# A two-layer hybrid backbone on one core: in the first layer's experts the down product also keeps its weights stationary, its result is turned back, and the expert loop is rotated by a third of gate and up

## The reference, cut to what matters

```python
def ec_moe(h, w_router, w_e_gate, w_e_up, w_e_down):
    cap = EC_CAPACITY * t // N_EXPERTS
    aff = jax.nn.softmax((h @ w_router).astype(jnp.float32), axis=-1)
    vals, idx = lax.top_k(jnp.swapaxes(aff, 1, 2), cap)
    xs = jax.vmap(lambda hb, ib: hb[ib])(h, idx)
    hid = jax.nn.silu(jnp.einsum('becd,edf->becf', xs, w_e_gate)) * jnp.einsum('becd,edf->becf', xs, w_e_up)
    ys = jnp.einsum('becf,efd->becd', hid, w_e_down) * vals[..., None].astype(h.dtype)
    return jax.vmap(lambda yb, ib: jnp.zeros((t, d), yb.dtype).at[ib.reshape(-1)].add(yb.reshape(-1, d)))(ys, idx)
```

## Time and profile before

| | us |
|---|---|
| median of 3 runs (4555.68 to 4568.88) | 4561.98 |
| the profiled execution, its own time | 4566.59 |
| its span in the trace | 4564.6 |
| first expert product of the first layer, start | 1644.95 |
| last expert product of the first layer ends | 2486.25 |

### The profile page before, as it was taken

The page is one execution under the profiler, slowest core; times in us unless marked ns, Lnnn a source line. Parts: engine busy times, 40 slices in busy tenths (PEclk is TensorE's granted clock), DMA queues, the critical chain, the costliest instruction groups (busy, mean ns, idle before and its releaser), DMA issues.

```text
span 4564.6 us, 62566 instructions
## 1 busy us (share of the span) xinstructions
PE 3719.1 (81%) x25844; PEld 2530.3 (55%) x25844; DVE 1174.9 (26%) x2798; ACT 730.7 (16%) x1485; POOL 111.0 (2%) x166
## 2 busy tenths in 40 slices
PE   6699888888989569999997568898878947877785
PEld 3355674656776347776775345655556634444442
DVE  0332321425640231111110243323246131110111
ACT  2221222002211200000000221312022120010101
POOL 0000000000000000000000000000000000000000
PEclk9799898898999679999999678898878969999997
DMA  4172101001011159999997200110100219999996
GB/s 175 64 272 80 39 33 51 10 24 41 24 51 56 46 206 341 345 347 345 339 348 268 81 23 24 58 46 28 42 24 24 79 74 332 378 383 381 380 374 255
DMA packets 326203, 740.21 MB, mean 162 GB/s; under 512 B 7456, under 2 KB 79136, under 8 KB 325936
## 3 DMA queue, kind: packets, MB, share of 16 engines
q1 hardware_dynamic: 314704, 695.29, 41.8%
q0 software_dynamic: 11360, 43.05, 3.3%
HBM read 713.09 MB, written 25.21 MB: 162 GB/s over the span
## 4 chain that ended last, share of the span: by engine, by line
PE 64%; DMA 16%; DVE 11%; ACT 5%; issue 3%; DVEq 0%; ACTq 0%; SPq 0%; POOL 0%; POOLq 0%
PE bank L526 11%; PE bank L910 8%; PE bank L464 7%; PE bank L883 7%; PE bank L457 5%; DMA ring<-in_w_e_up 4%; PE bank L874 4%; DMA ring<-in_w_e_gate 4%; PE bank L800 3%; ACT work L986 3%; DMA ring<-in_w_e_down 3%; DVE work L1401 3%; PE bank L616 3%; DMA f_rows<-work,idx 3%; PE bank L528 2%
## 5 line engine op out<-in xcount | busy, mean ns | idle before, releaser
L526 PE MATMUL bank<-HT,ring 128*128 128x256 f32 x2560 | 636.7, 405 | 16.8 <-DVEq L1442 12.6
L526 PEld LDWEIGHTS bank<-HT,ring 128*128 128x128 f32 x2560 | 516.5, 205 | 133.5 <-issue 39.5
L874 PE MATMUL bank<-ring,work 128*64 128x256 f32 x1536 | 391.3, 414 | 129.7 <-DMA ring<-in_w_e_up 67.6
L910 PE MATMUL bank<-ring,work 128*96 128x512 f32 (+1 forms) x1408 | 468.0, 598 | 25.8 <-DMA ring<-in_w_e_down 24.3
L883 PE MATMUL bank<-work,ring 128*64 128x96 f32 x11264 | 483.7, 249 | 3.7 <-DVEq L1921 3.0
L883 PEld LDWEIGHTS bank<-work,ring 128*64 128x64 f32 x11264 | 477.3, 139 | 16.6 <-issue 16.0
L875 PE MATMUL bank<-ring,work 128*64 128x256 f32 (+1 forms) x1536 | 375.7, 385 | 0.0
L874 PEld LDWEIGHTS bank<-ring,work 128*64 128x64 f32 x1536 | 221.5, 149 | 270.9 <-DMA ring<-in_w_e_up 85.9
L471 PE MATMUL bank<-const,work 128*128 128x128 f32 (+1 forms) x828 | 155.9, 338 | 233.9 <-DVEq L1429 52.8
L910 PEld LDWEIGHTS bank<-ring,work 128*96 128x96 f32 (+1 forms) x1408 | 166.0, 150 | 291.5 <-issue 255.4
L464 PE MATMUL bank<-ring,HT 128*128 128x512 f32 (+2 forms) x960 | 309.1, 486 | 0.0
(11 more groups left out here) (165 smaller groups left out, 3331.8 us busy)
## 6 DMA issues: line engine op xcount, KB each, us to landing
ring<-in_w_e_gate SPq DMA_DIRECT2D x64, 2048.0 KB, 10.5
ring<-in_w_e_up SPq DMA_DIRECT2D x64, 2048.0 KB, 10.1
ring<-in_w_e_down SPq DMA_DIRECT2D x64, 2048.0 KB, 9.7
ring<-in_w_ada SPq DMA_DIRECT2D x24, 2048.0 KB, 8.1
ring<-in_w_e_gate SPq DMA_DIRECT2D x32, 1536.0 KB, 10.1
ring<-in_w_e_up SPq DMA_DIRECT2D x32, 1536.0 KB, 8.2
ring<-in_w_e_down SPq DMA_DIRECT2D x32, 1536.0 KB, 10.0
ring<-in_w_gate SPq DMA_DIRECT2D x16, 2048.0 KB, 8.5
```

The lines of the kernel that those rows point to most:

```text
L526: pe.matmul(b[:, 0:256], w[:, k, d4 * P:(d4 + 1) * P], HT[:, k, off:off + 256], start=(k == 0), stop=(k == KD - 1))
L874: pe.matmul(b[0:64, 0:256], e_xs[:, k, 0:64], w[:, k, 0:256], start=(k == 0), stop=(k == KD - 1))
L910: ins = pe.matmul(banks[6 + half][lo:lo + cap, :], e_hidT[:, at, 0:cap], w[:, k, half * 512:half * 512 + 512], start=(f == 0), stop=(f == ...
```

## The change

Only the first layer's expert stage changes; the second layer's code is taken apart from it and issues what it issued.

- **Down.** `wide_down` keeps the weights stationary, like gate and up: for 8 output blocks `m` and 11 hidden blocks `f`, two halves of 64 columns, with the 96 tokens moving. The result comes out turned: output feature on the partitions, 4 x 96 columns in each of banks 6 and 7. It is 352 matmul records where there were 44.
- **Turning back.** ScalarE and VectorE copy the two banks (128x384 each) to `e_yT`, which lies over the unused `e_hid`. `turn_y` makes 8 transposes (stationary 128x96, moving 128x128) into banks 4 and 5, and from there the scaled copies to `e_ys` are as before.
- **Rotation.** Gate and up of group 0 of expert 0 stand ahead of the loop. A pass is: gate and up 1, `choose`, gate and up 2, `turn_rows`, down 0 to 2, gate and up 0 of the *next* expert, `turn_y`. VectorE and ScalarE are rotated alike.

```diff
+                def pairs(b, c0, w, k, c, x, start, stop):
+                    for half in range(2):
+                        ins = pe.matmul(b[64 * half:64 * half + 64, c0:c0 + cap], w[:, k, c + 64 * half:c + 64 * half + 64], x,
+                                        start=start, stop=stop, skip_group_check=True)
+                    return ins
...
+                def wide_down(e, i):
+                    wpiece(e, 6 + i)
+                    kk = EXP_DOWN[i]
+                    w = slot(n0 + 6 + i, 1024, kk)
+                    for m in range(KD):
+                        for k in range(kk):
+                            f = 4 * i + k
+                            ins = pairs(banks[6 + m // 4], (m % 4) * cap, w, k, m * P, e_hidT[:, f, 0:cap],
+                                        f == 0 and m % 4 == 0, f == NF - 1)
+                    ins.then_inc(sems["ys"], 1)
+                def turn_y():
+                    pe.wait_ge(sems["yt_a"], c.nth("yt_a"))
+                    pe.wait_ge(sems["yt_d"], c.nth("yt_d"))
+                    pe.wait_ge(sems["ys_a"], c.nth("ys_a"))
+                    pe.wait_ge(sems["ys_d"], c.nth("ys_d"))
+                    for m in range(KD):
+                        ins = pe.transpose(banks[4 + m // 4][0:cap, (m % 4) * P:(m % 4 + 1) * P], e_yT[:, m, :], ident)
+                    ins.then_inc(sems["y_t"], 1)
+                def wide_expert(e, last):
+                    wide_gate_up(e, 1)
+                    pe.wait_ge(sems["hid_f"], c.nth("hid_f"))
+                    if not last:
+                        choose()
+                    wide_gate_up(e, 2)
+                    pe.wait_ge(sems["hid_f"], c.nth("hid_f"))
+                    if not last:
+                        pe.wait_ge(sems["idx_next"], c.nth("idx_next"))
+                        turn_rows()
+                    wide_down(e, 0)
+                    wide_down(e, 1)
+                    pe.wait_ge(sems["hid_f"], c.nth("hid_f"))
+                    wide_down(e, 2)
+                    if not last:
+                        pe.wait_ge(sems["xs"], c.nth("xs"))
+                        wide_gate_up(e, 0, 1)
+                    turn_y()
...
+                def wide_expert(last):                      # ScalarE
+                    hidden(1)
+                    hidden(2)
+                    act.wait_ge(sems["ys"], c.nth("ys", 3))
+                    copy(e_yT[:, 0:4, :], banks[6][:, 0:4 * cap].rearrange("p (m j) -> p m j", m=4))
+                    act.sem_inc(sems["yt_a"], 1)
+                    if not last:
+                        hidden(0)
+                    act.wait_ge(sems["idx_now"], c.nth("idx_now"))
+                    act.wait_ge(sems["y_t"], c.nth("y_t"))
+                    do(e_ys[0:cap, 0:512], banks[4][0:cap, :], AF.Copy, scale=s_sel[0:cap, 1:2])
+                    act.sem_inc(sems["ys_a"], 1)
...
+                def wide_expert(e, last):                   # VectorE
+                    if not last:
+                        select(e + 1)
+                    hidden(1)
+                    if not last:
+                        next_chosen()
+                    hidden(2)
+                    if not last:
+                        tokens()
+                    dve.wait_ge(sems["ys"], c.nth("ys", 3))
+                    copy(e_yT[:, 4:8, :], banks[7][:, 0:4 * cap].rearrange("p (m j) -> p m j", m=4))
+                    dve.sem_inc(sems["yt_d"], 1)
+                    if not last:
+                        hidden(0)
+                    dve.wait_ge(sems["y_t"], c.nth("y_t"))
+                    ts(e_ys[0:cap, 512:1024], banks[5][0:cap, :], s_sel[0:cap, 1:2], ALU.mult)
+                    dve.sem_inc(sems["ys_d"], 1)
+                    if not last:
+                        dve.wait_ge(sems["scat"], c.nth("scat", 16))
+                        now_chosen()
```

More of the change, by code:

```diff
@@ new lines, in wide_gate_up @@
+                def wide_gate_up(e, g, ahead=0):
+                    for u in range(2):
+                        wpiece(e, 2 * g + u, ahead)
+                        n = EXP_W[2 * g + u]
+                        w = slot(n0 + 2 * g + u, n)
+                        b = banks[(0, 2, 0)[g] + u]
+                        for f in range(n // P):
+                            for k in range(KD):
+                                ins = pairs(b, f * cap, w, k, f * P, e_xs[:, k, 0:cap], k == 0, k == KD - 1)
+                        ins.then_inc(sems["gu"], 1)
@@ L891, in turn_hidden @@
                         b = banks[(4, 5, 4)[g]]
-                        for j in range(2 if two else 0):
+                        for j in range(2):
                             rows = P if 4 * g + 2 + j < NF else 64
@@ L918, in expert @@
                     gate_up(1)
[L919 to L922, removed]
+                    turn_hidden(0)
                     gate_up(2)
@@ L926, in expert @@
                         pe.wait_ge(sems["idx_next"], c.nth("idx_next"))
[L927 to L930, removed]
+                    turn_hidden(1)
                     if not last:
@@ L944, in moe @@
                 pe.wait_ge(sems["idx_next"], c.nth("idx_next"))
[L945 to L951, removed]
+                per = {"xs": 1, "sel": 1, "idx_next": 1, "rows_in": 16, "ys_a": 1, "ys_d": 1, "hid_f": 3}
+                if two:
+                    with pe.Fori(0, NE - 1) as e:
+                        c.begin(e, per | {"hid": 3})
+                        expert(e, False)
+                        c.e = None
+                    c.finish_loop(NE - 1)
+                    expert(NE - 1, True)
+                else:
+                    pe.wait_ge(sems["xs"], c.nth("xs"))
+                    wide_gate_up(0, 0)
+                    with pe.Fori(0, NE - 1) as e:
+                        c.begin(e, per | {"yt_a": 1, "yt_d": 1})
+                        wide_expert(e, False)
+                        c.e = None
+                    c.finish_loop(NE - 1)
+                    wide_expert(NE - 1, True)
                 pe.wait_ge(sems["ys_a"], c.nth("ys_a"))
@@ L1347, in expert @@
                     act.sem_inc(sems["ys_a"], 1)
-                act.sem_inc(sems["ys_a"], 1)
[L1350 to L1355, removed]
+                def wide_expert(last):
[10 more added lines that the diff above has]
+                    act.sem_inc(sems["ys_a"], 1)
+                act.sem_inc(sems["ys_a"], 1)
+                if cap == 64:
+                    with act.Fori(0, NE) as e:
+                        c.begin(e, {"gu": 6, "idx_now": 1, "ys": 3, "act_order": 8, "hid_t": 3})
+                        expert()
+                        c.e = None
+                    c.finish_loop(NE)
+                else:
+                    hidden(0)
+                    with act.Fori(0, NE - 1) as e:
+                        c.begin(e, {"gu": 6, "idx_now": 1, "ys": 3, "y_t": 1, "act_order": 5})
+                        wide_expert(False)
+                        c.e = None
+                    c.finish_loop(NE - 1)
+                    wide_expert(True)
                 for t in QT:
```

57 lines of the change are left out of this document (28 added, 29 removed).

## The result

| | before | after |
|---|---|---|
| median, us | 4564.72 (4 runs) | 4621.72 (4 runs, 4619.66 to 4625.87) |
| ratio | | 1.013, 95% interval 1.0115 to 1.0146 |
| profiled span | 4564.6 | 4617.7 |
| first layer's expert stage | 841.3 | 893.5 (1642.36 to 2535.8) |

I had forecast 4537. The stage is 52.2 us longer and the span 53.1, so nearly all of it lies in the stage. Windows of the changed kernel, columns as in the earlier trace rows: the loop, the second layer, and one stretch behind the loop's end.

The account below looks back on a forecast made before the run. TensorE's own work and one short wait were taken to bound the first layer's time. The stage would save 49 us, less 24 for fetching loop code: 25 off 4561.98 gives 4537 us, range 4507 to 4574.

Parts of the forecast that it names:

- The code of the loop: TensorE's first-layer loop body, 8.6 packets, is fetched again each pass: 1.6 us a pass, 24 us over 15 passes.
- The wait of `choose`: TensorE's wait for VectorE before `choose` stays about 1.9 us a pass under the rotation.
- The branch stops TensorE: Rival: at the loop's end TensorE stops for a code fetch, up to 6.8 us; kernel put at 4600, chance 0.12.
- wait for the gather: Before `turn_rows`, with only `gate_up(2)` ahead of it: 0.2 us a pass, bounds 0 and 1.0.
- ring: Some weight pieces come just in time for TensorE in the loop: 0.2 us a pass, bounds 0 and 2.
- stops in line: Code packets fetched within the pass at 0.23 us each: 1.6 us a pass after `choose` hides two.
- the clock's other falls: Slower-clock stretches of TensorE's products in the loop, taken as before: 0.71 us a pass.
- the 4.3 us that down saves: Down's products in a pass go from 18.98 to 14.64 us, saving 4.34.
- the hidden copies: Copies to `e_yT`, about 0.55 us each, lie beside the next expert's `gate_up(0)`; only the last expert pays, some 0.8 us.
- the body of 8.6 packets would not stay: The new loop body of 2168 instructions exceeds TensorE's instruction memory and is fetched each pass; the opposite rival had 0.25.
- The rotation: Moving the next expert's `gate_up(0)` to the pass's end leaves the wait before `choose` unchanged: nothing gained or lost.
- a body of 6 of them stays: The old loop body, 6 packets of 16 KB and 253 instructions each, runs without being fetched again.

Follow-up runs that it names:

- light queues: Changed kernel with only the first block of rows of each first-layer expert weight piece transferred; 4528.53 us in a single execution.
- the straight version: Changed kernel with TensorE's first-layer loop of 15 passes written out as straight code; 4577.07 us, ratio 1.0014.
- `turn_rows` late: Rotation alone with old down, and `turn_rows` moved behind `down(0)`; 4547.26 us, ratio 0.9953.
- whole weights: Changed kernel with down's weights loaded as whole 128 columns, one product in place of two halves; 4695.22 us, ratio 1.0277.
- quarter, shifted: Rotated loop with a quarter of down's output columns in the new form, plus 50 idle increments ahead of the loop; 4633.92 us, ratio 1.0134.
- 11 increments: Kernel before the change with 11 idle semaphore increments ahead of each of down's 22 products in the first layer's loop; 4890.4 us, ratio 1.0706.

## Why the prediction was wrong

**The step that failed** is in "The code of the loop": "a packet's own transfer is 0.6% of 16 engines over 53 us by 5, 1.0 us, and behind it `choose` leaves 1.9 us, so I take nothing". The stop is 4.5 us on the mean of 14 passes. A packet's time on the engines says how long it is moved, not how long TensorE is without code: even with light queues the stop is 2.2 us. The wait of `choose` did hide 1.9 of it, as said; but behind the stop came a fall of the clock, 2.0 us a pass, for which the forecast had no term. That is my rival "The branch stops TensorE", to which I gave 0.12; its reference row, the gather's 6.8 us, was nearer than the one I used. At 5 us it had put 4598, at 6.8 us 4625. By its own sum 4.5 us give 4590; the measured 4622 is more, since the fall of the clock took 2.0 us a pass, not 1.0, and the gather 1.4 more than forecast, while the stops in line took 1.3 less. The 4600 at which I put the rival was nearer than its sum deserved.

A pass, from one `turn_y` to the next, us:

| | forecast | measured |
|---|---|---|
| down's 352 products, at full clock | 14.64 | 14.74 |
| `turn_y` | 0.96 | 1.08 |
| stop at the loop's end | 0 | 4.50 |
| `gate_up(1)` | 10.65 | 12.67 |
| wait before `choose` | 1.9 | 0 |
| wait for the gather | 0.2 | 22.2 / 14 = 1.59 |
| ring | 0.2 | (3.1 + 1.9) / 14 = 0.36 |
| stops in line | 1.6 | (66.9 - 63.0) / 14 = 0.28 |
| the pass | 49.73 + 1.6 = 51.33 | 791.49 / 14 = 56.54 |

The lines add up to 5.1 of the 5.2 us between the two; the clock's other falls, which are what all pieces leave of the 56.54, came to about 0.7, as forecast.

**Right by its own steps:** the 4.3 us that down saves, the price of `turn_y`, the hidden copies, the ring, and that the body of 8.6 packets would not stay (10 packets a pass against my 9). The rotation did more than I gave it: I had it at nothing, and in a loop without `turn_y` it takes the wait before `choose` away whole.

**Right for a reason that needs mending:** "a body of 6 of them stays". Bodies of 1551 to 1733 instructions touching 7 blocks ran their passes without being fetched again; 1792 and 1834, and 1733 from a later start, touching 8, were fetched again. What decides is the number of blocks touched, with the bound between 7 and 8. The Trainium skill (Runtime: NRT & Kernel Launch, section Instruction fetch mechanics) gives TensorE a memory of 2048 instructions, which are 8 blocks. No loop of 8 blocks stayed here, so that size is no safe bound for a loop. It isn't contradicted either: a fetched pass moved about one packet more than its blocks, and if that is the block behind the loop, a loop of 7 fills 8; no run separates this from a memory of 7. Another sentence of the same section of the Trainium skill, which reckons with 32 KiB, has only two blocks held; for TensorE the silent passes of the 7-block loops contradict it.

**Mis-sized:** the gather, which I had landing after 6.8 us (bounds 0 to 1.0 for the wait), lands after 8.4 and makes 1.59. In line, the fetches cost 2.7 us a pass over 8.5 packets, 0.32 each, in the straight version, where I had taken 0.23; in the changed kernel, which has the long stops, it is 0.28 us a pass in all.

**Left open.** Why a body of 8 blocks is fetched every pass in some kernels and every second in another. Whether the turned down would bring its 3.3 us a pass if its code were held: the one version that was held turned a quarter and gained nothing over the rotation, for a reason seen only in part; the new down without the rotation wasn't run; and with `turn_rows` late the pass already met the weights at 51.4 us. How the 2.2 us that remain under light queues divide. And why the stops beside full queues differ (4.5, 5.4, 6.1 to 7.2 us in three kernels).

## What to carry to other kernels

Count the instructions of a loop that a change lengthens (a product that becomes eight also becomes eight weight loads) and the 16 KB blocks it touches from where it begins; in these runs 7 stayed and 8 did not, and the price beside dense weight queues was a stop of 2.7 to 7.2 us in each fetched pass, and mostly a fall of the clock behind it: more than the 3.3 us that this edit was to bring. See in the DMA queues whether the instruction queue is silent through the loop, before anything else. Where an edit has two halves, run each alone: here the half that I had put at nothing was the gain (0.5%) when run alone, and the loss came when the other was added to it.

## What the runs showed of the hardware

- A loop on TensorE that touches 7 blocks of 256 instructions (1551 to 1733 instructions) ran without being fetched again; one that touches 8 or 9 (1733 from a later start to 2186) was fetched again in every pass or in every second, with about one packet more than its blocks.
- The stop behind the branch back to such a loop: 4.5 us on the mean in the changed kernel, 5.4 (whole weights), 6.1 to 7.2 (quarter, shifted), 2.7 to 3.2 (11 increments), and 2.0 to 2.6 in the changed kernel with light queues.
- Shifting a loop of 1733 instructions by 50 made it be fetched again in every second pass: +79 us, about 7 of them the 50 increments that shifted it.
- Straight code is not free either beside full weight queues: 0.7 to 1.4 us at a block in the last expert, 0.82 us on the mean of a stop in the straight version.
- The transfer of 96 gathered rows landed after 4.1 us with light queues, 6.8 in the kernel before, 8.4 in the changed one.
- An idle semaphore increment on TensorE takes 0.15 us; 8 ahead of each product of down made it 1.22 us long in place of 0.86.
